# A hybrid attention layer on one core: second weight quarter loaded by rows, square of tile 3 moved to ScalarE, start-up work reordered

## The chip, the core and the metric

The kernel runs on one core of one Trainium2 chip. The metric is the device time of one execution in microseconds, median over repeated runs.

## What is computed

One decoder layer on x of 512 x 1024 (float32), cut to what matters:

```python
h = rmsnorm(x, norm_pre_g)                      # per row, over 1024
u = h @ w_in                                    # 1024 x 4096
dq, dk, dv, dg, mq, mk, mv, mg = split(u)       # 512 columns each
A = diff_attention(dq, dk, dv, lam, bias)       # 4 heads, two softmax maps, p0 - lam * p1, rmsnorm per head
B = moba_attention(mq, mk, mv, bias)            # 8 heads; at 512 rows all causal blocks are taken
y = concat(A * silu(dg), B * silu(mg)) @ w_out
out = x + rmsnorm(y, norm_post_g)
```

## The kernel before

The rows of x are four tiles of 128 (t = 0 to 3), the 1024 inner columns eight rows of blocks (k = 0 to 7). A unit is one 128 x 512 result of the projections: 32 units for `w_in` and 8 for `w_out`, in the order of the table `ORDER`. Products are made in float16 pairs: each operand is split into a high and a low half (`w_hi`, `w_lo`; `ht[:, 0]`, `ht[:, 1]`), and three products are summed in PSUM (high with high, high with low, low with high). The weights come in quarters of two rows k, 512 KB each, into `stage` (four places): `load_quarter(n)` on SyncE, but the second quarter (n = 1) by ScalarE's queue. ScalarE makes the high half (`split`, L748 and L749), VectorE the low one (L910, L912, or one row with `split_row`, L899). SyncE loads a place again when both halves are made (`split_lo`), and for quarters 4 to 6 also when TensorE has read it (`first_read`).

The start is different for each tile:
- Tile 0 / unit 0 doesn't wait for its norm. TensorE turns the raw rows (L539), VectorE weighs them by the norm's gains (`x_weigh`, L1001), and `first_quarter` (L592) multiplies float32 weights straight from `stage`, quarter by quarter; the factor 1/rms of tile 0 (`first_scale`) is put on at the eviction (`unit(0)`, L771 on ScalarE, L954 on VectorE).
- Tile 1: the square of its left half on ScalarE (`x_square`, L735), of its right half on VectorE (`x_half_square`, L963), their sum on VectorE (`x_mean_square`, L971), its reciprocal root on POOL (L481), `x_norm(1)` on VectorE (L977). TensorE turns the rows after the third quarter of unit 0 (L539, waits for `xs_ready`); ScalarE takes the high half from PSUM (`x_hi(1)`, L788), VectorE the low one (`x_lo(1)`, L1012).
- Tiles 2 and 3: squares, sum and root in the same way, then ScalarE writes the high half of the normed rows (`xn_hi`, L823, waits for the root), VectorE the low one (`xn_lo`, L1018), and SyncE turns each with a DMA transpose (`turn_x`, L400) into `ht`.

Units 1 to 3 run in `late_lower_unit`: 16 matmuls with the high half of the tile (L611), then 8 with the low one (L618), so that the low half is wanted only later. Units from 4 on (`unit_quarter`, L581) want all four tiles. After seven units the attention steps are mixed with further units, in slots set by tables; TensorE then multiplies to the end, and rows are normed and stored.

Within an engine the order is that in which the program is written. On SyncE the first loads are: tile 0, quarter 0, tile 1, quarter 2 (waits for tile 0), quarter 3 (waits for quarter 0), tile 2 (waits for `w_loaded[1]`, the second quarter), tile 3 (waits for tile 1), quarters 4 and 5, then the four transposes (both high halves, then both low ones), quarters 6 to 8. ScalarE's order there is `x_square(0)`, `split(0)`, `x_square(1)`, `split(1)` to `split(3)`, `x_square(2)`, `x_hi(1)`, `x_square(3)`, `xn_hi(2)`, `unit(0)`, `xn_hi(3)`.

Of the kernel before, what the change touches and what calls it, by code (L numbers as in the profile page):

```python
# [7 lines left out]
def bass_hymba_diff_moba_layer(  # L8
# [25 lines left out]
    ALU = mybir.AluOpType  # L34
# [145 lines left out]
    with ctx:  # L180
# [99 lines left out]
        rows_stored = sem("rows_stored")  # L280
        strips_loaded = [sem(f"strips_loaded{r}") for r in range(2)]
        w_loaded = [sem(f"w_loaded{i}") for i in range(4)]
        xres_loaded = [sem(f"xres_loaded{t}") for t in range(TILES)]
        stored = [sem(f"stored{i}") for i in range(2)]
        stored_last = sem("stored_last")
# [72 lines left out]
        def _(sp):  # L358
# [59 lines left out]
            load_quarter(5)  # L418
            with nc.allow_non_contiguous_dma(reason="32 x 12 table, transposed once"):
                sp.dma_start(rel_t, rel_bias.rearrange("b h -> h b")).then_inc(rel_loaded, 16)  # L420
            for h in range(2):
                for t in range(2, TILES):
                    turn_x(t, h)
            load_quarter(6)
            load_quarter(7)
# [44 lines left out]
        @block.gpsimd  # L470
        def _(pool):
            nc.gpsimd.memset(ident[:, :], 0.0).then_inc(ident_zero, 1)
            nc.gpsimd.memset(minus_half[:, :], -0.5).then_inc(consts_ready, 1)
            pool.wait_ge(ident_zero, 1)
            nc.gpsimd.affine_select(out=ident[:, :], in_=ident[:, :], compare_op=ALU.not_equal, fill=1.0,
                                    base=0, pattern=[[-1, P]], channel_multiplier=1).then_inc(consts_ready, 1)
            pool.wait_ge(consts_ready, 2)

            for t in range(TILES):
                pool.wait_ge(x_mean, t + 1)  # L480
                nc.gpsimd.tensor_tensor(x_rstd[:, t:t + 1], x_ms[:, t:t + 1], minus_half[:, 0:1],  # L481
                                        ALU.pow).then_inc(x_rstd_ready, 1)
                if t == 0:
                    pool.wait_ge(x_rstd_ready, 1)
                    nc.gpsimd.tensor_scalar(first_scale[:, :], x_rstd[:, 0:1], U_SCALE, 1.0, ALU.mult,
                                            ALU.mult).then_inc(first_scale_ready, 1)

            nc.gpsimd.memset(row_sb[:, 0:P - 1], MASKED).then_inc(row_masked, 1)
            pool.wait_ge(rel_loaded, 16)
            for b in range(BUCKETS):  # L490
                lo = first_distance(b)
                hi = first_distance(b + 1) if b + 1 < BUCKETS else SEQ + 1
                last = nc.gpsimd.tensor_copy(row_sb[:, P - 1 + lo:P - 1 + hi],
                                             rel_t[:, b:b + 1].to_broadcast([HEADS, hi - lo]))
                if b == BUCKETS - 1:
                    last.then_inc(row_built, 1)
            pool.wait_ge(subln_loaded, 16)


            keep = (1.0 - LAMBDA_INIT) ** 2  # L500
            for c in range(DIFF_HEADS):
                pool.wait_ge(sub_squared, TILES * (c + 1))
                nc.gpsimd.tensor_scalar(sub_ms[:, c, :], sub_sq[:, c, :], 1.0 / (2 * DH * keep),  # L503
                                        SUBLN_EPS / keep, ALU.mult, ALU.add).then_inc(sub_mean, 1)
                pool.wait_ge(sub_mean, c + 1)
                nc.gpsimd.tensor_tensor(sub_rstd[:, c, :], sub_ms[:, c, :], minus_half[:, :],
                                        ALU.pow).then_inc(sub_rstd_ready, 1)
                pool.wait_ge(sub_rstd_ready, c + 1)
                rows = gates[:, 0, :, c * P:(c + 1) * P]
                nc.gpsimd.tensor_tensor(rows, rows, sub_rstd[:, c, :].unsqueeze(2).to_broadcast([P, TILES, P]),  # L510
                                        ALU.mult).then_inc(sub_scaled, 1)
                pool.wait_ge(sub_scaled, c + 1)
                nc.gpsimd.tensor_tensor(rows, rows, subln[:, :].unsqueeze(1).to_broadcast([P, TILES, P]),
                                        ALU.mult).then_inc(diff_normed, 1)

            for t in range(TILES):
                i = t
                pool.wait_ge(y_squared, 2 * i + 1)
                nc.gpsimd.tensor_scalar(y_part[:, t:t + 1], y_sq[:, t, 0:1], NORM_EPS * W_SCALE ** 2, 1.0,
                                        ALU.add, ALU.mult).then_inc(y_part_ready, 1)  # L520
                pool.wait_ge(y_part_ready, i + 1)
                pool.wait_ge(y_squared, 2 * (i + 1))
                if t < TILES - 1:
                    nc.gpsimd.tensor_tensor(y_ms[:, t:t + 1], y_sq[:, t, 1:2], y_part[:, t:t + 1],
                                            ALU.add).then_inc(y_mean, 1)
                else:
                    nc.gpsimd.tensor_tensor(y_most[:, :], y_sq[:, t, 1:2], y_part[:, t:t + 1],
                                            ALU.add).then_inc(y_most_ready, 1)
                pool.wait_ge(y_mean, i + 1)
                nc.gpsimd.tensor_tensor(y_rstd[:, t:t + 1], y_ms[:, t:t + 1], minus_half[:, 0:1],  # L530
                                        ALU.pow).then_inc(y_rstd_ready, 1)
# [3 lines left out]
        def _(pe):  # L535
# [50 lines left out]
            def first_quarter(q):  # L586

                pe.wait_ge(x_first_ready, q // 2 + 1)
                pe.wait_ge(w_loaded[q], 16)
                for k in (2 * q, 2 * q + 1):  # L590
                    cols = slice(k % 2 * WIDTH, (k % 2 + 1) * WIDTH)
                    last = nc.tensor.matmul(unit_ps[:, 0, :], x_first[:, k, :], stage[:, q, cols], start=(k == 0),  # L592
                                            stop=(k == KT - 1))
                last.then_inc(first_read if q < 3 else unit_done, 1)
# [132 lines left out]
        def _(act):  # L727
# [10 lines left out]
            def split(n):  # L738

                g, k = n // 4, 2 * (n % 4)  # L740
                act.wait_ge(w_loaded[n % 4], 16 * (n // 4 + 1))
                if g >= 3:
                    act.wait_ge(unit_done, LAST_OF_GROUP[g - 3] + 1)
                src = stage[:, n % 4, :].rearrange("p (k n) -> p k n", k=2)
                if g < len(GROUPS):
                    if n == 0:
                        act.wait_ge(g_scaled, 1)
                    nc.scalar.activation(w_hi[:, g % 3, k, :], src[:, 0, :], ACT.Copy, scale=g_cols[:, k:k + 1])  # L748
                    nc.scalar.activation(w_hi[:, g % 3, k + 1, :], src[:, 1, :], ACT.Copy,  # L749
                                         scale=g_cols[:, k + 1:k + 2]).then_inc(split_hi, 1)  # L750
                else:
                    nc.scalar.activation(w_hi[:, g % 3, k:k + 2, :], src, ACT.Copy,
                                         scale=W_SCALE).then_inc(split_hi, 1)
# [72 lines left out]
            def x_square(t):  # L826
                act.wait_ge(x_loaded[t], 16)

                square(x_sq[:, t:t + 1], x_sb[:, t, 0:DM // 2], x_squared, t + 1)

            nc.scalar.dma_start(g_rows[:, :], norm_pre_g[0].rearrange("(k p) -> k p", p=P)).then_inc(gpre_loaded, 16)  # L831
            first = GROUPS[0][2]
            nc.scalar.dma_start(stage[:, 1, :].rearrange("p (k n) -> p k n", k=2),
                                w_in_v[:, 2:4, first:first + WIDTH]).then_inc(w_loaded[1], 16)
            x_square(0)
            split(0)
            x_square(1)
# [2 lines left out]
            split(3)  # L840
            x_square(2)
            x_hi(1)
            x_square(3)
            xn_hi(2)
            unit(0)
            xn_hi(3)
            for u in range(1, FIRST_UNITS):
                if u > 2:
# [1 line left out]
                        split(n)  # L850
                    unit(u)
                if u == 1:
                    split(4)
                    unit(1)
                    split(5)
                    x_hi(0)
# [36 lines left out]
        def _(dve):  # L893
            def split_row(n, part):

                g, k = n // 4, 2 * (n % 4) + part
                dve.wait_ge(split_hi, n + 1)
                src = stage[:, n % 4, part * WIDTH:(part + 1) * WIDTH]
                ins = nc.vector.scalar_tensor_tensor(w_lo[:, g % 3, k, :], src, g_cols[:, k:k + 1],  # L899
                                                     w_hi[:, g % 3, k, :], ALU.mult, ALU.subtract)  # L900
# [221 lines left out]
            split(0)  # L1122
            x_half_square(1)
            x_mean_square(1)
            x_norm(1)
            split(1)
            split_row(2, 0)
            x_half_square(2)
            x_mean_square(2)
            split_row(2, 1)  # L1130
            x_half_square(3)
            x_mean_square(3)
            split(3)
            x_lo(1)
            unit(0)
            xn_lo(2)
            xn_lo(3)
            for u in range(1, FIRST_UNITS):
                if u > 2:
# [2 lines left out]
                unit(u)  # L1142
                if u == 1:
                    x_scale()
                    split(4)
                    split(5)
                if u == 2:
                    x_lo(0)
                    split(6)
                if u == 3:  # L1150
                    dve.wait_ge(lam_loaded, 16)
                    dve.wait_ge(x_half_squared, TILES)
                    for i in range(2):
                        nc.vector.tensor_tensor_reduce(out=heads_out[:, i * DH:(i + 1) * DH],
                                                       in0=lam_in[:, 2 * i, :], in1=lam_in[:, 2 * i + 1, :],
# [70 lines left out]
```

## Time and profile before

| | |
|---|---|
| median of 3 runs | 253.86 us (253.48 to 253.91) |
| the profiled execution's own time | 253.41 us |
| its span on the core | 251.6 us |
| granted TensorE clock | 0.997 of full speed |
| busy | TensorE 244.8 us (97%), VectorE 178.4 us (71%), ScalarE 142.9 us (57%), POOL 30.1 us (12%) |
| DMA queues | 42.47 MB, mean 169 GB/s |

The times of single instructions come from the profiled execution, whose span leaves out some 1.8 us around the recorded work. Start times are counted from the start of the span. The ends of matmuls are modelled, and neighbouring matmuls overlap in the records, so that starts say more than durations. PEld is TensorE's weight load; a name with q (SPq) is an engine's queue, here for the instruction that issues a DMA.

### The profile page before, as it was taken

The numbers are of one execution on the slowest core, as the hardware profiler recorded it, in microseconds if no ns is written. First come the engines' busy times: TensorE is split into PE (matmuls) and PEld (weight loads), VectorE is DVE, ScalarE is ACT, GpSimd is POOL, SyncE is SP. The second block draws the span as 40 slices with busy tenths as digits, with TensorE's granted clock in tenths as the row PEclk, the third lists the DMA queues.
The fourth block names the chain that finished last, engine by engine and source line by source line (L and its number), as shares of the span: only waits on it lengthen the run. The fifth ranks groups of instructions, "written<-read, shape, count | busy, mean of one in ns | idle before, by whom it ended". The sixth has DMA issues, their size and how long they took to land.

```text
span 251.6 us, 4449 instructions
## 1 busy us (share of the span) xinstructions
PE 244.8 (97%) x1564; PEld 122.5 (49%) x1564; DVE 178.4 (71%) x396; ACT 142.9 (57%) x336; POOL 30.1 (12%) x73
## 2 busy tenths in 40 slices
PE   8999999999999999999999999999999999999991
PEld 7444444445444554544455444454444444555570
DVE  3899786587477788868777767968788896835313
ACT  3894675274456666574676595577566655611110
POOL 1267000000000410040041032000000000111101
PEclk9999999999999999999999999999999999999998
DMA  7978989605765545443935553577749876982422
GB/s 262 389 225 188 315 261 375 193 5 135 107 182 141 181 115 145 139 157 106 208 96 137 147 161 112 131 199 179 179 102 199 202 182 155 198 208 42 125 86 83
DMA packets 59674, 42.47 MB, mean 169 GB/s; under 512 B 45808, under 2 KB 46072, under 8 KB 59652
## 3 DMA queue, kind: packets, MB, share of 16 engines
q1 hardware_dynamic: 59364, 41.66, 62.0%
q10 hardware_dynamic: 288, 0.53, 0.6%
q8 instruction: 13, 0.21, 0.4%
q14 instruction: 9, 0.07, 0.1%
HBM read 29.04 MB, written 2.13 MB: 124 GB/s over the span
## 4 chain that ended last, share of the span: by engine, by line
PE 94%; DMA 3%; issue 1%; DVE 0%; DVEq 0%; ACTq 0%; ACT 0%; POOLq 0%; POOL 0%
PE unit_ps L581 73%; PE score_ps L637 6%; PE o_ps L658 5%; PE unit_ps L611 4%; DMA stage<-in_w_in_dram 3%; PE unit_ps L592 2%; PE unit_ps L618 2%; PE unit_ps L712 1%; PE score_ps L712 1%; PE score_ps L539 0%; DVE area L1107 0%; DVEq L180 0%; ACTq L831 0%; ACT junk L735 0%; POOLq L180 0%
## 5 line engine op out<-in xcount | busy, mean ns | idle before, releaser
L581 PE MATMUL unit_ps<-area,w_hi 128*128 128x512 f16 x256 | 76.3, 380 | 0.0
L796 ACT ACTIVATE arena<-arena,negmax 128x512 f32<-128x512 f32 (+3 forms) x64 | 35.4, 554 | 50.0 <-DVE negmax L1034 49.9
L581 PE MATMUL unit_ps<-w_hi,area 128*128 128x512 f16 x192 | 60.3, 380 | 0.0
L581 PE MATMUL unit_ps<-area,w_lo 128*128 128x512 f16 x128 | 48.6, 379 | 0.0
L581 PEld LDWEIGHTS unit_ps<-area,w_hi 128*128 128x128 f16 x256 | 24.0, 98 | 27.3 <-issue 1.1
L581 PE MATMUL unit_ps<-w_lo,area 128*128 128x512 f16 x96 | 36.4, 379 | 0.0
L1034 DVE CUSTOM_DVE_ANT_0 arena<-score_ps,strips 128x512 f32<-128x512 f32 (+3 forms) x64 | 28.6, 485 | 9.4 <-PE score_ps L637 9.4
L910 DVE SCALAR_TENSOR_TENSOR w_lo<-stage,g_cols,w_hi 128x512 f16<-128x512 f32 x31 | 23.7, 765 | 10.1 <-ACT w_hi L749 10.1
L581 PEld LDWEIGHTS unit_ps<-w_hi,area 128*128 128x128 f16 x192 | 18.8, 98 | 21.9 <-issue 1.2
L748 ACT ACTIVATE w_hi<-stage,g_cols 128x512 f16<-128x512 f32 x32 | 22.7, 710 | 4.0 <-DMA stage<-in_w_in_dram 4.0
L912 DVE SCALAR_TENSOR_TENSOR w_lo<-stage,g_cols,w_hi 128x512 f16<-128x512 f32 x31 | 24.1, 778 | 0.0
L749 ACT ACTIVATE w_hi<-stage,g_cols 128x512 f16<-128x512 f32 x32 | 22.6, 707 | 0.0
L1063 DVE TENSOR_TENSOR arena<-arena 128x512 f16<-128x512 f32 (+5 forms) x32 | 21.0, 656 | 1.5 <-ACT arena L810 1.5
L810 ACT ACTIVATE arena<-arena 128x512 f16<-128x512 f32 (+5 forms) x32 | 19.0, 592 | 3.6 <-DVE arena L1054 3.5
L581 PE MATMUL unit_ps<-w_hi,q_hi 128*128 128x512 f16 x64 | 19.9, 380 | 0.0
L581 PEld LDWEIGHTS unit_ps<-area,w_lo 128*128 128x128 f16 x128 | 12.5, 98 | 15.1
L658 PE MATMUL o_ps<-v_hi,pt 128*128 128x64 f16 (+1 forms) x240 | 18.9, 202 | 0.0
L658 PEld LDWEIGHTS o_ps<-v_hi,pt 128*128 128x128 f16 x240 | 15.5, 98 | 3.8
L735 ACT ACTIVATE junk<-unit_ps 128x512 f16<-128x512 f32 (+1 forms) x8 | 4.5, 564 | 22.6 <-PE unit_ps L581 22.0
L658 PE MATMUL o_ps<-v_lo,pt 128*128 128x64 f16 (+1 forms) x120 | 16.2, 202 | 0.0
L581 PE MATMUL unit_ps<-w_hi,q_lo 128*128 128x512 f16 x48 | 14.9, 379 | 0.0
L503 POOL TENSOR_SCALAR sub_ms<-sub_sq 128x4 f32<-128x4 f32 x4 | 0.8, 193 | 113.2 <-ACT junk L735 113.2
(114 smaller groups left out, 356.7 us busy)
## 6 DMA issues: line engine op xcount, KB each, us to landing
stage<-in_w_in_dram SPq DMA_DIRECT2D x31, 512.0 KB, 4.0
stage<-in_w_out_dram SPq DMA_DIRECT2D x8, 512.0 KB, 4.2
arena<-in_x_dram SPq DMA_DIRECT2D x4, 512.0 KB, 5.0
strips<-bias_rows SPq DMA_DIRECT2D x4, 512.0 KB, 4.8
stage<-in_x_dram SPq DMA_DIRECT2D x4, 512.0 KB, 4.1
out_dram<-area SPq DMA_DIRECT2D x3, 512.0 KB, 2.7
strips<-bias_rows SPq DMA_DIRECT2D x1, 1024.0 KB, 8.0
stage<-in_w_in_dram ACTq DMA_DIRECT2D x1, 512.0 KB, 6.9
```

Source lines behind the costliest of these rows:

```text
L581: last = nc.tensor.matmul(bank, a, b, start=(k == 0 and n == 0), stop=(k == KT - 1 and n == 2))
L611: nc.tensor.matmul(bank, ht[:, 0, k, rows], b[:, g % 3, k, :], start=(k == 0 and b is w_hi), stop=False)
L637: last = nc.tensor.matmul(score_ps[:, bank, col:col + n], a[part, ch, rows], b[part, ch, 0:n], start=first, stop=final)
L658: last = nc.tensor.matmul(o_ps[:, o % 2, col:col + width], a, b[:, k, src], start=(k == 0 and n == 0), stop=(k == t and n == 2))
L748: nc.scalar.activation(w_hi[:, g % 3, k, :], src[:, 0, :], ACT.Copy, scale=g_cols[:, k:k + 1])
L749: nc.scalar.activation(w_hi[:, g % 3, k + 1, :], src[:, 1, :], ACT.Copy, scale=g_cols[:, k + 1:k + 2]).then_inc(split_hi, 1)
L796: nc.scalar.activation(probs[:, i % 2, m, 0:n], probs[:, i % 2, m, 0:n], ACT.Exp, bias=negmax[:, i, m:m + 1], scale=-1.0, accum_out=sums[: ...
L810: nc.scalar.activation(hi, probs[:, i % 2, 0:1 + r, 0:n], ACT.Copy).then_inc(p_hi_ready, 1)
L910: nc.vector.scalar_tensor_tensor(w_lo[:, g % 3, k, :], src[:, 0, :], g_cols[:, k:k + 1], w_hi[:, g % 3, k, :], ALU.mult, ALU.subtract)
L912: nc.vector.scalar_tensor_tensor(w_lo[:, g % 3, k + 1, :], src[:, 1, :], g_cols[:, k + 1:k + 2], w_hi[:, g % 3, k + 1, :], ALU.mult, ALU.s ...
L1034: nc.vector.tensor_tensor_reduce(out=probs[:, i % 2, m, 0:n], in0=score_ps[:, bank, col:col + n], in1=strips[:, h, 0:n][:, ::-1], scale=-1 ...
L1063: nc.vector.tensor_tensor(lo, probs[:, i % 2, 0:1 + r, 0:n], hi, ALU.subtract)\
```

## The change

- The second quarter is loaded by two DMAs of one row each, both on ScalarE's queue: row 2 counts on `row_loaded`, row 3 on `w_loaded[1]`. TensorE waits for each row by itself. ScalarE's `split(1)` waits for both, and signals its first row by `row_split`.
- VectorE's low half of row 2, `split_row(1, 0)`, runs ahead of `x_norm(1)`, row 3 behind it; quarter 2 is split whole ahead of tile 2's half square.
- The square of tile 3 is made by ScalarE alone over 1024 columns, and POOL adds the epsilon; VectorE's `x_half_square(3)` and `x_mean_square(3)` go.
- ScalarE runs `unit(0)` ahead of `xn_hi(2)`, and `x_square(3)` and `split(4)` ahead of `xn_hi(3)`; VectorE runs `split(4)` between `xn_lo(2)` and `xn_lo(3)`.
- SyncE transposes tile by tile (high and low half of tile 2, then of tile 3).

```diff
@@ SyncE, transposes
-            for h in range(2):
-                for t in range(2, TILES):
+            for t in range(2, TILES):
+                for h in range(2):
                     turn_x(t, h)
@@ POOL
             for t in range(TILES):
+                if t == TILES - 1:
+                    pool.wait_ge(x_squared, TILES)
+                    nc.gpsimd.tensor_scalar(x_ms[:, t:t + 1], x_sq[:, t:t + 1], NORM_EPS, 1.0, ALU.add,
+                                            ALU.mult).then_inc(x_mean, 1)
                 pool.wait_ge(x_mean, t + 1)
@@ TensorE, first_quarter
-                pe.wait_ge(w_loaded[q], 16)
                 for k in (2 * q, 2 * q + 1):
+                    pe.wait_ge(row_loaded if k == 2 else w_loaded[q], 16)
@@ ScalarE, split
+                if n == 1:
+                    act.wait_ge(row_loaded, 16)
                 act.wait_ge(w_loaded[n % 4], 16 * (n // 4 + 1))
...
-                    nc.scalar.activation(w_hi[:, g % 3, k, :], src[:, 0, :], ACT.Copy, scale=g_cols[:, k:k + 1])
+                    row = nc.scalar.activation(w_hi[:, g % 3, k, :], src[:, 0, :], ACT.Copy,
+                                               scale=g_cols[:, k:k + 1])
+                    if n == 1:
+                        row.then_inc(row_split, 1)
@@ ScalarE, x_square
-                square(x_sq[:, t:t + 1], x_sb[:, t, 0:DM // 2], x_squared, t + 1)
+                cols = DM // 2 if t < TILES - 1 else DM
+                square(x_sq[:, t:t + 1], x_sb[:, t, 0:cols], x_squared, t + 1)
@@ ScalarE, start
-            nc.scalar.dma_start(stage[:, 1, :].rearrange("p (k n) -> p k n", k=2),
-                                w_in_v[:, 2:4, first:first + WIDTH]).then_inc(w_loaded[1], 16)
+            nc.scalar.dma_start(stage[:, 1, 0:WIDTH], w_in_v[:, 2, first:first + WIDTH]).then_inc(row_loaded, 16)
+            nc.scalar.dma_start(stage[:, 1, WIDTH:2 * WIDTH], w_in_v[:, 3, first:first + WIDTH])\
+                .then_inc(w_loaded[1], 16)
...
             x_square(2)
             x_hi(1)
+            unit(0)
+            xn_hi(2)
             x_square(3)
-            xn_hi(2)
-            unit(0)
+            split(4)
             xn_hi(3)
@@ VectorE, split_row
-                dve.wait_ge(split_hi, n + 1)
+                if part == 0:
+                    dve.wait_ge(row_split, 1)
+                else:
+                    dve.wait_ge(split_hi, n + 1)
@@ VectorE, start
             x_mean_square(1)
+            split_row(1, 0)
             x_norm(1)
-            split(1)
-            split_row(2, 0)
+            split_row(1, 1)
+            split(2)
             x_half_square(2)
             x_mean_square(2)
-            split_row(2, 1)
-            x_half_square(3)
-            x_mean_square(3)
             split(3)
             x_lo(1)
             unit(0)
             xn_lo(2)
+            split(4)
             xn_lo(3)
```

`split(4)` is taken out of its old place, after unit 1, on both engines.

How VectorE's instructions stand around the norm of tile 1 and the sum of tile 2, before (from the half square of tile 1; ISA is the half square and the read of its sum, `stage` with `w_hi` a split):

```order
L963 ISA heads_out,x_half_sq<-arena 128x512 [waits x_half_squared,x_loaded1]
L963 ISA x_half_sq 128x1
L971 TENSOR_TENSOR x_ms<-x_sq,x_half_sq 128x1 [waits x_half_squared,x_squared]
L977 TENSOR_SCALAR arena<-arena,x_rstd 128x1024 [waits x_rstd_ready]
L910 SCALAR_TENSOR_TENSOR w_lo<-stage,g_cols,w_hi 128x512 [waits split_hi]
L912 SCALAR_TENSOR_TENSOR w_lo<-stage,g_cols,w_hi 128x512
L899 SCALAR_TENSOR_TENSOR w_lo<-stage,g_cols,w_hi 128x512 [waits split_hi]
L963 ISA heads_out,x_half_sq<-arena 128x512 [waits x_half_squared,x_loaded2]
L963 ISA x_half_sq 128x1
L971 TENSOR_TENSOR x_ms<-x_sq,x_half_sq 128x1 [waits x_half_squared,x_squared]
L899 SCALAR_TENSOR_TENSOR w_lo<-stage,g_cols,w_hi 128x512 [waits split_hi]
L963 ISA heads_out,x_half_sq<-arena 128x512 [waits x_half_squared,x_loaded3]
```

The same place in the changed kernel:

```order
L979 ISA heads_out,x_half_sq<-arena 128x512 [waits x_half_squared,x_loaded1]
L979 ISA x_half_sq 128x1
L987 TENSOR_TENSOR x_ms<-x_sq,x_half_sq 128x1 [waits x_half_squared,x_squared]
L915 SCALAR_TENSOR_TENSOR w_lo<-stage,g_cols,w_hi 128x512 [waits row_split]
L993 TENSOR_SCALAR arena<-arena,x_rstd 128x1024 [waits x_rstd_ready]
L915 SCALAR_TENSOR_TENSOR w_lo<-stage,g_cols,w_hi 128x512 [waits split_hi]
L926 SCALAR_TENSOR_TENSOR w_lo<-stage,g_cols,w_hi 128x512 [waits split_hi]
L928 SCALAR_TENSOR_TENSOR w_lo<-stage,g_cols,w_hi 128x512
L979 ISA heads_out,x_half_sq<-arena 128x512 [waits x_half_squared,x_loaded2]
L979 ISA x_half_sq 128x1
L987 TENSOR_TENSOR x_ms<-x_sq,x_half_sq 128x1 [waits x_half_squared,x_squared]
L926 SCALAR_TENSOR_TENSOR w_lo<-stage,g_cols,w_hi 128x512 [waits split_hi]
```

One split now stands between the sum of tile 1 and its norm; between that norm and the half square of tile 2 there are three splits, as before.

ScalarE from the square of tile 2 to the first split of the fifth quarter, before (`v_hi` is the eviction of unit 0, `pt` the high half of a normed tile):

```order
L735 ACTIVATE junk,x_sq<-arena 128x512 [waits x_squared,x_loaded2]
L788 ACTIVATE area<-score_ps 128x8x128 [waits xt_ready]
L735 ACTIVATE junk,x_sq<-arena 128x512 [waits x_squared,x_loaded3]
L823 ACTIVATE pt<-arena,x_rstd 128x1024 [waits x_rstd_ready]
L771 ACTIVATE v_hi<-unit_ps,first_scale 128x512 [waits first_scale_ready,unit_done]
L823 ACTIVATE pt<-arena,x_rstd 128x1024 [waits x_rstd_ready]
L748 ACTIVATE w_hi<-stage,g_cols 128x512 [waits w_loaded0]
```

And in the changed kernel:

```order
L741 ACTIVATE junk,x_sq<-arena 128x512 [waits x_squared,x_loaded2]
L799 ACTIVATE area<-score_ps 128x8x128 [waits xt_ready]
L782 ACTIVATE v_hi<-unit_ps,first_scale 128x512 [waits first_scale_ready,unit_done]
L834 ACTIVATE pt<-arena,x_rstd 128x1024 [waits x_rstd_ready]
L741 ACTIVATE junk,x_sq<-arena 128x1024 [waits x_squared,x_loaded3]
L756 ACTIVATE w_hi<-stage,g_cols 128x512 [waits w_loaded0]
L760 ACTIVATE w_hi<-stage,g_cols 128x512
L834 ACTIVATE pt<-arena,x_rstd 128x1024 [waits x_rstd_ready]
```

The first two stand as they did; the eviction has gone ahead of tile 2's high half, and tile 3's square (now of 1024 columns) and the split ahead of tile 3's.

## Rows read from the trace of the kernel before

**Rows 1.** Busy time by stage: us, each engine's busy us (x instructions), clock, DMA share, GB/s.

```profile
0.00:14.60 14.60, 13.28 (x52) 8.62 (x53) 8.99 (x22) 9.49 (x17) 2.67 (x11) 1.00 0.89 326
14.60:30.00 15.40, 15.40 (x73) 6.96 (x73) 14.47 (x21) 9.89 (x15) 8.04 (x35) 1.00 0.84 223
```

**Rows 2.** Waits of TensorE, whole program: waited for, us in total, times, longest.

```profile
PE unit_ps L546 <- PEq L1214: 0.8, 1, 0.8
PE unit_ps L592 <- DMA stage<-in_w_in_dram: 0.3, 1, 0.3
PE unit_ps L592 <- DVE gates L1001: 0.2, 1, 0.2
```

**Rows 3.** Timeline of TensorE: start us, us, engine, line, tile, xcount [idle before <-releaser].

```profile
6.15 1.95 PE L592 MATMUL unit_ps<-stage,gates 128*128 128x512 f32 x4 [0.24 <-DVE gates L1001]
8.42 3.67 PE L592 MATMUL unit_ps<-stage,gates 128*128 128x512 f32 x8 [0.31 <-DMA stage<-in_w_in_dram]
11.93 1.04 PE L539 MATMUL score_ps<-ident,arena 128*128 128x128 f32 x8
...
12.91 1.88 PE L592 MATMUL unit_ps<-stage,gates 128*128 128x512 f32 x4
...
14.53 0.10 PEld L611 LDWEIGHTS unit_ps<-w_hi,area 128*128 128x128 f16 x1 [0.57 <-ACT area L788]
14.63 0.38 PE L611 MATMUL unit_ps<-w_hi,area 128*128 128x512 f16 x1
...
19.59 0.10 PEld L611 LDWEIGHTS unit_ps<-w_hi,area 128*128 128x128 f16 x1
19.81 0.38 PE L611 MATMUL unit_ps<-w_hi,area 128*128 128x512 f16 x1
```

**Rows 4.** Chain of waits, its first transfer: start us, us, what.

```profile
1.34 6.94 DMA stage<-in_w_in_dram
```

**Rows 5.** Timeline of ScalarE, 12 to 17 us.

```profile
12.85 0.63 ACT L735 ACTIVATE junk<-arena 128x512 f16<-128x512 f32 x1 [0.35 <-DMA arena<-in_x_dram]
...
13.47 1.00 ACT L788 ACTIVATE area<-score_ps 128x1024 f16<-128x1024 f32 x1
...
15.09 1.15 ACT L823 ACTIVATE pt<-arena,x_rstd 128x1024 f16<-128x1024 f32 x1
```

**Rows 6.** Timeline of SyncE's DMA issues.

```profile
4.27 2.14 SPq L373 DMA_DIRECT2D stage<-in_w_in_dram  x2
8.30 0.82 SPq L404 DMA_DIRECT2D arena<-in_x_dram  x2
...
16.26 1.33 SPq L400 DMA_TRANSPOSE area<-pt  x1
```

**Rows 7.** DMA issues at 4.27, 8.30, 16.26 us: KB, us from issue to landing.

```profile
stage<-in_w_in_dram SPq DMA_DIRECT2D x1, 512.0 KB, 5.3
...
arena<-in_x_dram SPq DMA_DIRECT2D x1, 512.0 KB, 4.5
...
area<-pt SPq DMA_TRANSPOSE x1, 3.2
```

**Rows 8.** Timeline of VectorE around the norm of tile 1 and the sum of tile 2.

```profile
10.37 0.76 DVE L977 TENSOR_SCALAR arena<-arena,x_rstd 128x1024 f32<-128x1024 f32 x1 [0.67 <-POOL x_rstd L481]
...
13.02 0.69 DVE L963 CUSTOM_DVE_ANT_0 heads_out<-arena 128x512 f32<-128x512 f32 x1
...
13.82 0.16 DVE L971 TENSOR_TENSOR x_ms<-x_sq,x_half_sq 128x1 f32<-128x1 f32 x1
13.90 0.74 DVE L899 SCALAR_TENSOR_TENSOR w_lo<-stage,g_cols,w_hi 128x512 f16<-128x512 f32 x1
```

**Rows 9.** Timeline of POOL: the reciprocal roots of tiles 1 to 3.

```profile
9.78 0.55 POOL L481 TENSOR_TENSOR x_rstd<-x_ms,minus_half 128x1 f32<-128x1 f32 x1 [2.58 <-DVE x_ms L971]
14.06 0.99 POOL L481 TENSOR_TENSOR x_rstd<-x_ms,minus_half 128x1 f32<-128x1 f32 x1 [3.73 <-DVE x_ms L971]
15.60 0.99 POOL L481 TENSOR_TENSOR x_rstd<-x_ms,minus_half 128x1 f32<-128x1 f32 x1 [0.55 <-DVE x_ms L971]
```

More of the change, by code:

```diff
@@ L282, in bass_hymba_diff_moba_layer @@
         w_loaded = [sem(f"w_loaded{i}") for i in range(4)]
+        row_loaded = sem("row_loaded")
+        row_split = sem("row_split")
         xres_loaded = [sem(f"xres_loaded{t}") for t in range(TILES)]
@@ L852, in _ @@
                 if u == 1:
-                    split(4)
                     unit(1)
@@ L1144, in _ @@
                     x_scale()
-                    split(4)
                     split(5)
@@ L1151, in _ @@
                     dve.wait_ge(lam_loaded, 16)
-                    dve.wait_ge(x_half_squared, TILES)
+                    dve.wait_ge(x_half_squared, TILES - 1)
                     for i in range(2):
```

## The prediction

> **What bounds the kernel now.** I read the table of stages first. In the first 14.6 us TensorE is busy for 13.28 us; from 14.6 to 30.0 us it is busy for all 15.40 us [rows 1], and its whole list of waits has three entries, all before that: 0.8 us at the start, 0.2 us on VectorE and 0.3 us on a DMA, both at L592, the first unit [rows 2]. So from 14.63 us on TensorE sets the time: what moves the start of a later matmul moves the end by as much, and what any other engine gains there is worth nothing unless TensorE waits for it. The change touches the first 25 us.
>
> The list hides how close the waits are, because a matmul's row reaches over the next one (0.38 us long, one started every 0.216 us: 24 of them from 14.63 to 19.81 us). Starts tell more [rows 3]. The first unit's matmuls start every 0.43 us (four of them run from 12.91 to 14.34 and the next work starts at 14.63 = 12.91 + 4 x 0.43). The first quarter, from 6.15 us, is therefore through at 7.87 us, and the second starts at 8.42 us: TensorE really stands still for 0.55 us. It waits for the second quarter, issued by ScalarE's queue at 1.34 us and landed 6.94 us later, at 8.28 us [rows 4].
>
> Two other things end just in time, and they decide this case:
> - Unit 1's first weight load starts at 14.53 us, released by ScalarE's high half of tile 1 (13.47 to 14.47 us); its matmul at 14.63 us is also the moment at which TensorE has come through. ScalarE was late because tile 2's rows landed at 12.85 us, and their square (0.63 us) stands ahead of that half [rows 3, 5].
> - Unit 2's first weight load at 19.59 us needs the transpose of tile 2's upper half. SyncE issued it at 16.26 us, and it took 3.2 us: landed at 19.46 us [rows 3, 6, 7]. The margin is 0.13 us. That transpose waited for xn_hi(2) (15.09 to 16.24 us), which waited for POOL's reciprocal root (ended 15.05 us), which waited for x_ms(2), started by VectorE at 13.82 us [rows 5, 8, 9].
>
> **The second quarter by rows.** The stall of 0.55 us goes if row 2 is there at 7.87 us and row 3 at 8.73 us. The same bytes move beside the same other transfers; row 3 is issued one issue (about 0.4 us) later. I bound row 2's landing between 4.27 us (when tile 0, issued first of all, released SyncE [rows 6]) and 8.28 us. The second and third quarters landed 1.29 us apart (8.28 and 4.27 + 5.3 = 9.57 us [rows 6, 7]), so a half is worth about 0.65 us: I take 7.6 us for row 2, and for row 3 the old 8.28 us, since its last byte has the same traffic ahead of it; its bounds are 7.6 and 8.93 us. The extra issue on ScalarE's queue lies before tile 0 is there. The second quarter is then through at 9.59 us; the third landed at 9.57 us, just in time, and ends at 11.31 us. So TensorE comes 0.55 us sooner to the transposes of tile 1. ScalarE still waits for both rows (split(1) has both waits), behind tile 1's square: nothing changes for it up to split(3).
>
> **What gives it back, twice.** First, VectorE now runs split_row(1, 0) between x_mean_square(1) and x_norm(1), in the 0.67 us in which it waited for POOL's root [rows 8]. That looks free. But look at the root: 0.55 us where VectorE waited (9.78 us), 0.99 us both times when VectorE went on with a split (14.06 us, the split 0.16 us earlier [rows 8], and 15.60 us, behind tile 3's sum) [rows 9]. In the changed kernel the split follows x_ms(1) as the one at 13.90 us follows x_ms(2), so it starts at about 9.62 us and the root at 9.78 us: the same distance, so I take 0.99 us. The root ends at 10.77 instead of 10.33 us, and x_norm(1) runs from 10.81 to 11.57 us: 0.44 us late. The transposes, wanted at 11.38 us, start at about 11.77 us instead of 11.93 us, and TensorE is through with the fourth quarter at 14.46 us instead of 14.63 us: 0.17 us are left of 0.55. The bounds of the root are 0.55 and 0.99 us.
>
> The Trainium skill, SBUF — State Buffer, section "Who interferes with whom", has the rule for it: a VectorE instruction with two inputs in SBUF holds off a GpSimd instruction that reads SBUF. Its section "A bandwidth-pool intuition that's wrong (but worth ruling out)" puts the end of such a block at about 115 ns behind the end of VectorE's instruction. An estimate by it: the root would end at 9.62 + 0.74 + 0.12 = 10.48 us and the delay be 0.15 us. The row of 14.06 us says otherwise: that split ended at 14.64 us, the root at 15.05 us, 0.41 us behind; the row decides.
>
> Second, unit 1 still needs ScalarE's half of tile 1, behind the square of tile 2. Tile 2's load is issued as before when w_loaded[1] is there (8.28 us), 4.5 us to landing [rows 7]: 12.85 us, square, half until 14.47 us, first matmul at 14.63 us. **The gain is 0.** If tile 2 landed sooner ScalarE could begin at 12.50 us; TensorE's own 14.46 us then lets 0.17 us through.
>
> **The term that remains.** VectorE's row of work behind x_norm(1) is as long as before: one split has gone ahead of it and one is added (split(2) whole), so three splits lie between it and the half square of tile 2. All is shifted by 0.44 us: half square from 13.46 instead of 13.02 us, x_ms(2) from 14.26 instead of 13.82 us. Tile 2's rows (12.85 us) and ScalarE's square (about 13.5 us) are there. A split follows again, so the root is 0.99 us, from 14.50 to 15.49 us; xn_hi(2) runs from 15.53 to 16.68 us; the transpose is issued at 16.70 us and lands at 19.90 us at 3.2 us. Matmuls started 0.14 us behind the landing of the second quarter (8.28, 8.42), and a weight load with its matmul started 0.06 + 0.10 us behind ScalarE's half (14.47, 14.53, 14.63): unit 2 starts at 20.04 to 20.14 instead of 19.81 us. Term: +0.23 to +0.33 us; I take **+0.25 us**, and 0 if the root keeps 0.55 us. Since transposes no longer follow so closely behind this one, 3.0 us might do, which gives +0.05 us.
>
> **Edits that cost nothing.** unit(0) ahead of xn_hi(2) on ScalarE fits in the gap: TensorE's unit ends at about 14.6 us, and an eviction of 512 columns (about 0.7 us, like the half square) at 15.3 us, before the root (15.49 us). With an undisturbed root at 15.05 us TensorE would also be 0.39 us further ahead, and the eviction would run from the end of ScalarE's half (14.47 us) to about 15.1 us. Tile 3's square by ScalarE: 1024 columns, 1.15 us by the row of xn_hi(2) [rows 5] for 0.63 us, and 0.7 us less on VectorE; with POOL's added sum, root and split(4) (two of about 0.7 us) ahead of xn_hi(3), its half ends at about 20.5 us and its transpose lands at 23.7 us, wanted by unit 3 at 19.81 + 24 x 0.216 = 24.99 us. Lower half: VectorE ends it at about 21.8 us, landed at 25.0, wanted at 28.4 us. SyncE's order by tiles is no worse: the lower half of tile 2 goes at about 18.9 us. The fifth split comes earlier, quarter 8 is issued sooner, and nobody waits for it. All covers are TensorE's 15.40 us of uninterrupted work.
>
> **Sum.** The profiled execution took 253.41 us (span 251.6): 253.41 - 0.55 + 0.55 (given back) + 0.25 = 253.66 us. It lies 0.45 us under the median of 253.86 us; from the median: **254.1 us**. A measurement of this kernel can tell some 0.2% (0.5 us) from no change.
>
> **Rivals.**
> 1. The forecast, unit 2 late by its transpose, +0.05 to +0.33 us: 253.9 to 254.2 us. Chance 0.57.
> 2. The root isn't stretched, or only by 0.15 us. For: only two long rows, and another cause may have made them. With 0.15 us the transpose of tile 2 lands at 19.61 us and unit 2 is late by at most 0.05 us: 253.9 us. (This is what the Trainium skill's SBUF page, cited above, would make of it.) Without any, x_norm(1) is on time, and if tile 2 also lands earlier, because row 3's semaphore comes before 8.28 us, ScalarE starts at 12.50 us and the gain is 0.35 us at unit 1, of which the eviction ahead of xn_hi(2) and the transpose let some 0.1 us through: 253.7 to 253.9 us. Chance 0.20; with case 1 it makes "no change" 0.77.
> 3. Slower: row 3 becomes the late one. Issued 0.41 us later, it may land at 8.7 us by that issue, or at 8.93 us by half a quarter's 1.29 us. SyncE waits for it before it loads tile 2, so that tile lands 0.4 to 0.65 us later, and unit 1 starts that much later, one for one (the transpose's lateness is then hidden): 254.3 to 254.5 us. It decides from 0.25 us on. For it: that wait is the last one ended before SyncE's issue at 8.30 us. Against: the bytes ahead of row 3 are no more. Chance of over 0.2% slower, with what a late transpose adds: 0.15.
> 4. Faster by over 0.2% needs the whole 0.55 us: tile 2 over 0.5 us sooner, an undisturbed root, and a sooner transpose at once. Chance 0.08.
>
> **Range.** From 253.5 us (case 2 with the spread of the runs below the median, 0.4 us) to 254.6 us (case 3).
>
> **What would show it.** In the changed kernel's profile: no wait of L592 on the stage DMA, the first unit's second quarter from about 7.9 us; the second root 0.99 us long; the transposes of tile 1 started between 11.7 and 11.8 us; unit 1 at 14.6 us, released by ScalarE's half; the first transpose of tile 2 issued at 16.7 us and a gap of 0.2 to 0.3 us in TensorE's starts before 20.1 us; nothing after it. I am wrong if unit 1 starts before 14.4 us or after 14.9 us, or if the gap before unit 2 isn't there, or if TensorE waits at a later unit.

## The result, and the profile after

The changed kernel took 254.74 us (median of 9 runs, 254.53 to 254.96) against 253.52 us for the kernel before (9 runs, 253.44 to 254.45): ratio 1.0040, 95% interval 1.0030 to 1.0051. It is slower by 1.2 us from median to median (0.8 to 1.3 us by the interval), and 254.74 us lies 0.14 us above the range that was given. The profiled execution is the slowest of the nine: 254.96 us, span 253.2 us, 1.6 us longer than the span of before.

The waits of TensorE in the whole program (columns as in [rows 2]):

```profile
PE unit_ps L598 <- DMA stage<-in_w_in_dram: 1.1, 1, 1.1
PE unit_ps L552 <- PEq L1228: 0.8, 1, 0.8
PE unit_ps L617 <- ACT area L799: 0.2, 1, 0.2
```

The wait of L592 (now L598) on the stage has not gone. It has grown from 0.3 to 1.1 us and moved: it was in front of the second quarter, and now it is in front of the first. TensorE's timeline of the start:

```profile
7.60 5.39 PE L598 MATMUL unit_ps<-stage,gates 128*128 128x512 f32 x12 [1.11 <-DMA stage<-in_w_in_dram]
13.06 1.09 PE L545 MATMUL score_ps<-ident,arena 128*128 128x128 f32 x8
...
14.10 1.88 PE L598 MATMUL unit_ps<-stage,gates 128*128 128x512 f32 x4
16.16 0.39 PE L617 MATMUL unit_ps<-w_hi,area 128*128 128x512 f16 x1 [0.17 <-ACT area L799]
```

Against [rows 3] the first quarter starts at 7.60 us instead of 6.15, and the three quarters then run without a gap (12 matmuls in 5.39 us). That is not yet the gain of the row-wise wait: the second quarter was wanted at 7.60 + 4 x 0.43 = 9.32 us and was whole at 9.35 us, so that even a wait for the whole quarter would have cost next to nothing. And unit 1 starts at 16.16 us instead of 14.63: 1.53 us of the 1.6 us. The chain of waits says why (start us, us, what):

```profile
1.74 7.61 DMA stage<-in_w_in_dram
9.35 0.02 issue
9.36 5.08 DMA arena<-in_x_dram
14.45 0.02 issue
14.47 0.03 ACT junk L741
14.49 0.51 issue
15.01 0.19 ACT junk L741
15.19 0.92 ACT area L799
16.11 0.05 issue
16.16 3.63 PE unit_ps L617 x16
```

Row 3 of the second quarter landed at 9.35 us, where the whole quarter had landed at 8.28 us [rows 4]. SyncE waits for it before it loads tile 2, which took 5.1 us and landed at 14.45 us instead of 12.85; its square and ScalarE's half of tile 1 follow, and then unit 1.

Row 3 was not the only late one. Three loads as KB and us to landing: the first quarter (`stage`, SPq, issued at 1.2 us), tile 1 (`arena`, 1.65 us) and row 2 (`stage`, ACTq, 1.34 us):

```profile
stage<-in_w_in_dram SPq DMA_DIRECT2D x1, 512.0 KB, 6.3
arena<-in_x_dram SPq DMA_DIRECT2D x1, 512.0 KB, 7.3
stage<-in_w_in_dram ACTq DMA_DIRECT2D x1, 256.0 KB, 5.9
```

The first quarter, which the change doesn't touch, landed at 7.5 us; ScalarE began its split at 6.04 us before and at 7.49 us now. So this is no matter of which load stands ahead: fewer bytes moved. The stretch from 4 to 7 us, before and then in the changed kernel (columns as in [rows 1]; the last three are clock, DMA share, GB/s of the whole core):

```profile
4.00:7.00 3.00, 2.76 (x16) 2.20 (x17) 2.26 (x7) 1.69 (x4) 0.64 (x2) 1.00 1.04 406
```

```profile
4.00:7.00 3.00, 2.49 (x14) 2.30 (x14) 1.83 (x6) 0.72 (x2) 0.14 (x1) 1.00 0.93 312
```

406 - 312 = 94 GB/s over 3 us are 0.28 MB, or 0.7 us at 406 GB/s. The DMA engines are still busy most of the time (share 0.93 for 1.04), but move a quarter less.

The part of the forecast on POOL holds to the hundredth. POOL's roots of tiles 1 and 2, and SyncE's first transpose:

```profile
11.23 0.99 POOL L487 TENSOR_TENSOR x_rstd<-x_ms,minus_half 128x1 f32<-128x1 f32 x1 [3.45 <-DVE x_ms L987]
15.95 0.99 POOL L487 TENSOR_TENSOR x_rstd<-x_ms,minus_half 128x1 f32<-128x1 f32 x1 [3.73 <-DVE x_ms L987]
```

```profile
18.14 6.54 SPq L402 DMA_TRANSPOSE area<-pt  x4
```

The root of tile 1 takes 0.99 us for 0.55 [rows 9]. The transpose is issued at 18.14 us and takes 3.1 us to 21.24 us; unit 2 needs it at 16.16 + 24 x 0.216 = 21.34 us and started at 21.36: as unit 1 is so late, this lateness is hidden.

### The profile page after: what moved, and what is told of

Read it like the earlier page. It is cut to its first block, busy times and chain, and to the rows that moved or that the text cites. A ratio compares the mean times of both kernels' runs of the same rounds, so it can differ in the third digit from the quotient of the medians.

```text
span 253.2 us, 4447 instructions
## 1 busy us (share of the span) xinstructions
PE 245.6 (97%) x1564; PEld 123.0 (49%) x1564; DVE 177.5 (70%) x393; ACT 143.4 (57%) x336; POOL 31.6 (12%) x74
## 4 chain that ended last, share of the span: by engine, by line
PE 91%; DMA 5%; issue 1%; ACT 1%; ACTq 0%; DVE 0%; DVEq 0%; POOLq 0%; POOL 0%
PE unit_ps L587 72%; PE score_ps L643 6%; PE o_ps L664 5%; PE unit_ps L617 4%; DMA stage<-in_w_in_dram 3%; PE unit_ps L624 2%; DMA arena<-in_x_dram 2%; PE unit_ps L718 1%; PE score_ps L718 1%; ACT area L799 0%; DVE area L1123 0%; ACT junk L741 0%; DVEq L180 0%; ACTq L843 0%; ACTq L845 0%
```

## The experiments

Ratios are against the kernel before, run on the same chip.

**Which half of the change costs.** e1 is the kernel before with the loading by rows and the waits on it alone; this is the edit of the load:

```diff
-            nc.scalar.dma_start(stage[:, 1, :]..., w_in_v[:, 2:4, ...]).then_inc(w_loaded[1], 16)
+            nc.scalar.dma_start(stage[:, 1, 0:WIDTH], w_in_v[:, 2, ...]).then_inc(row_loaded, 16)
+            nc.scalar.dma_start(stage[:, 1, WIDTH:2 * WIDTH], w_in_v[:, 3, ...]).then_inc(w_loaded[1], 16)
```

> The kernel before with the second quarter loaded by two DMAs of one row and the waits on them, and no other edit. Theory L (the loading form is the cost: the two DMAs disturb the first transfers, all land 0.9 to 1.6 us late, and tile 2's landing sets unit 1's start): DMA traffic dips between 5.0 and 6.5 us as in the changed kernel, the first quarter lands near 7.5 us instead of 6.0, tile 2 near 14.4 instead of 12.85 us, unit 1 starts near 16.1 us, +1.2 to +1.5 us. Theory O (the reordering of VectorE, ScalarE and SyncE is the cost): within 0.2 us of the kernel before.

Measured: 254.39 us against 253.69, ratio 1.0032 (1.0021 to 1.0042). In its profile the first quarter landed at 7.0 us and tile 2 at 13.66 us, and unit 1 started at 15.35 us:

```profile
4.00:7.00 3.00, 2.33 (x14) 2.14 (x14) 1.99 (x6) 0.73 (x3) 0.31 (x1) 1.00 1.00 312
```

```profile
15.35 0.39 PE L612 MATMUL unit_ps<-w_hi,area 128*128 128x512 f16 x1 [0.15 <-ACT area L791]
```

The same 312 GB/s. The direction and the mechanism are those of theory L, but the size, +0.7 us (0.5 to 1.1 us by the interval), is under the +1.2 us that it named.

e2 is the changed kernel with that load whole again (the diff of e1, reversed, in the changed kernel).

> The changed kernel with the second quarter loaded by one DMA again; all the reordering stays. Theory L: 0 to +0.3 us against the kernel before, unit 1 at 14.6 us, and unit 2 up to 0.3 us late by its transpose, as predicted (second root 0.99 us, transpose issued at 16.7 us). Theory O: +1.0 to +1.3 us.

Measured: 253.80 against 253.69 us, ratio 1.0001 (0.9992 to 1.0010); theory O falls. The reordering costs nothing that can be measured, traffic from 4 to 7 us is 397 GB/s, and the profile shows the term that was forecast. It also shows the first three quarters without a gap (12 matmuls in 5.42 us from 6.73 us), although the second one is loaded and waited for whole: the first quarter began 0.58 us later than before, so that the second was there when it was wanted. POOL's roots of tiles 1 and 2, SyncE's first transpose, TensorE before unit 2:

```profile
10.06 1.03 POOL L486 TENSOR_TENSOR x_rstd<-x_ms,minus_half 128x1 f32<-128x1 f32 x1 [2.24 <-DVE x_ms L983]
14.82 0.99 POOL L486 TENSOR_TENSOR x_rstd<-x_ms,minus_half 128x1 f32<-128x1 f32 x1 [3.73 <-DVE x_ms L983]
```

```profile
17.02 6.55 SPq L401 DMA_TRANSPOSE area<-pt  x4
```

```profile
18.15 1.89 PE L623 MATMUL unit_ps<-w_hi,area 128*128 128x512 f16 x8
20.24 0.38 PE L616 MATMUL unit_ps<-w_hi,area 128*128 128x512 f16 x1 [0.20 <-issue]
```

Eight matmuls of 0.216 us from 18.15 us end at 19.88 us; unit 2 starts at 20.24: a gap of 0.36 us behind a transpose issued at 17.02 us with 3.1 us to landing (20.12 us).

**Is it the number of loads, their size, or what they read?** e7 adds one load of 4 KB behind the whole second quarter, on the same queue.

```diff
+            nc.scalar.dma_start(spare[0:KT, :], norm_pre_g[0]...).then_inc(spare_loaded, 16)
```

> The kernel before with one more load of 4 KB on ScalarE's queue behind the second quarter (the norm's gains once more, into a spare tile). It adds a load and its completion but no bytes to speak of. If the number of loads is the cause: +0.8 us and a dip at 5 to 6 us. If it is the form by rows: within 0.3 us of before.

Measured: 253.75 against 253.69 us, ratio 0.9990 (0.9975 to 1.0004), 402 GB/s from 4 to 7 us. One more load and its completion, as small as this one, cost nothing.

e4 moves row 3 to SyncE's queue; e5 leaves both rows on ScalarE's and issues row 3 only after tile 0 has landed, at 4.2 us; e6 loads the first quarter by rows (SyncE's queue) and the second one whole.

> The kernel before with row 2 by ScalarE's queue and row 3 by SyncE's, behind tile 1. If what costs is that ScalarE's queue has two transfers beside SyncE's: tile 1 and the first quarter land as before (8.1, 6.0 us) and the time is within 0.3 us of the kernel before. If any loading by rows costs: +0.8 to +1.5 us.

> The kernel before with the second quarter by rows on ScalarE's queue, but row 3 issued only after tile 0's square (at about 4.6 us), so that no more than four loads are under way at once, as in the kernel before. If the number of loads under way in the first 4 us is what costs: no dip of the traffic at 5 to 6 us, first quarter landed near 6.0 us, time within 0.3 us of before or better. If a load of one row (256 KB, one 2 KB piece per partition) is itself slow: the dip stays and the time is 0.8 us or more over before.

> The kernel before with the first quarter (SyncE's queue) loaded by two DMAs of one row each and the second one whole. If any loading by rows costs, wherever it stands: a dip again and +0.5 us or more. If only a second load on ScalarE's queue beside SyncE's costs: within 0.3 us of before.

Measured: e4 254.74 us, 1.0043 (1.0030 to 1.0055); e5 254.45 us, 1.0018 (1.0004 to 1.0031); e6 255.02 us, 1.0045 (1.0031 to 1.0060), all against 253.69 us. Each has its dip: 190 GB/s in the sixth us in e4, 180 in e5, in e6 already 266 in the fifth. It comes on either queue and for either quarter. e5 doesn't settle the number of loads under way: from 4.2 us on it has five (first quarter, row 2, tile 1, third quarter, row 3) where the kernel before has four, not four as its expectation says. e11, below, does. The theory in e5's expectation that was right on the dip asked for 0.8 us or more; the interval gives 0.1 to 0.8 us.

The dip does not follow every load of one row, though. In e5 row 3 moves alone on ScalarE's queue (q10) between 7.5 and 9 us, nearly all of its 0.26 MB, and the traffic is whole; from 10.5 to 11.5 us, when row 3 has landed (9.99 us) and nothing moves on q10, it falls once more:

```profile
DMA packets 304, 0.62 MB, mean 411 GB/s; under 512 B 8, under 2 KB 8, under 8 KB 304
q10 hardware_dynamic: 119, 0.24, 41.0%
```

```profile
DMA packets 70, 0.15 MB, mean 148 GB/s; under 512 B 14, under 2 KB 14, under 8 KB 70
```

Row 3 moves without a dip in e1 (408 GB/s from 6.5 to 8.5 us) and in the changed kernel too (407 GB/s from 7 to 9 us). A second dip with no load of one row under way stands in e1 (147 GB/s from 11.0 to 11.5 us), e4 (246 in the twelfth us) and e6 (205 in the tenth) as well. In e4 tile 1 landed on time (8.15 us), and it didn't help: row 3 landed at 8.85 us, and unit 1 started at 15.40 us. e6's profiled run, its slowest at 257.16 us, also had TensorE's granted clock at 0.5 (1.2 GHz) from 9 to 12 us, after it had waited 1.9 us for the stage.

e10 divides another load of 512 KB in the same way: tile 1 in two halves of 512 columns, one 2 KB piece per partition, 4 KB apart in memory.

> The kernel before with tile 1 of x loaded by two DMAs of 512 columns (256 KB each, one 2 KB piece per partition, as a row of weights, but pieces 4 KB apart in memory instead of 16 KB). If a 256 KB load of one 2 KB piece per partition is slow whatever it reads: traffic dips to 200 to 270 GB/s somewhere between 5 and 8 us and +0.5 us or more. If the dip hangs on the weights' 16 KB distance: no dip, within 0.3 us of before.

Measured: 253.71 against 253.74 us, ratio 0.9993 (0.9981 to 1.0005). From 4 to 7 us:

```profile
4.00:7.00 3.00, 3.00 (x15) 2.88 (x16) 1.79 (x6) 1.95 (x4) 0.10 (x1) 1.00 1.01 378
```

So 256 KB in one 2 KB piece per partition are not slow as such: 378 GB/s, at least 363 in each us of that stretch, and no time lost.

e11 divides the second quarter again in two loads of 256 KB, by columns: both rows in each.

```diff
+            for c0, done in ((0, row_loaded), (WIDTH // 2, w_loaded[1])):
+                nc.scalar.dma_start(stage_kn[:, :, c0:c0 + WIDTH // 2],
+                                    w_in_v[:, 2:4, first + c0:first + c0 + WIDTH // 2]).then_inc(done, 16)
```

> The kernel before with the second quarter by two DMAs of 256 KB each that hold half of the columns of both rows (two 1 KB pieces per partition). If what costs is a load of one row only (all its pieces 16 KB apart): no such dip, at most what smaller pieces cost, within 0.5 us of before. If any division of the quarter into 256 KB loads costs: a dip at 5 to 6 us and +0.8 us or more.

Measured: 253.80 against 253.74 us, ratio 1.0006 (0.9992 to 1.0020). e11 differs from e1 in two things: what addresses a load reads, and that it has two pieces of 1 KB per partition. e12 separates them: rows again, but each row goes to the stage in two separated pieces (`pieces` is a view "p (c k n) -> p k c n" with c=2, k=2).

```diff
+            for k, done in ((0, row_loaded), (1, w_loaded[1])):
+                nc.scalar.dma_start(pieces(stage[:, 1, :])[:, k],
+                    w_in_v[:, 2 + k, first:first + WIDTH].rearrange("p (c n) -> p c n", c=2)).then_inc(done, 16)
```

> As e1, the second quarter by two loads of one row each on ScalarE's queue, but every row goes to the stage as two separated pieces of 256 columns, so that each load has two 1 KB pieces per partition, as many and as small as in e11; only the memory addresses differ from e11 (one row, all partitions 16 KB apart, instead of two rows in turn). If the addresses are what costs: traffic from 4 to 7 us near 310 GB/s as in e1 and +0.5 to +1.0 us. If the small number of pieces per load is (8 for each of the 16 DMA engines): near 380 GB/s as in e11 and within 0.3 us of before.

Measured: 254.37 against 253.79 us, ratio 1.0019 (1.0006 to 1.0032). The stage from 4 to 7 us, e11 and then e12:

```profile
4.00:7.00 3.00, 2.81 (x15) 2.62 (x16) 1.78 (x6) 1.93 (x4) 0.10 (x1) 1.00 1.03 378
```

```profile
4.00:7.00 3.00, 3.00 (x15) 3.00 (x16) 1.67 (x6) 2.03 (x4) 0.10 (x1) 1.00 0.88 295
```

Two loads of 256 KB in 1 KB pieces on the same queue in both; 378 GB/s where a load takes two rows in turn, 295 GB/s where it takes one. e11 has as many loads under way as e1 and e12, so their number isn't it. The engines' waits and reads of the second quarter differ as well, but up to 7 us none of them has begun. So the dip hangs on how the addresses are divided between the two loads: with rows each one reads 128 places 16 KB apart (a row of `w_in` is 4096 x 4 bytes). But such a load isn't slow in itself: row 3 of e12, from 7 to 8.5 us, moved at 391 GB/s for the whole core, as in e5. Why the first of them is caught, no run here shows.

**Halves by partitions.** e3 was meant to test the number of loads: two loads of 64 partitions.

> The kernel before with the second quarter loaded by two DMAs of 64 partitions each, both rows in each, so that the number of DMAs is that of the changed kernel but not their shape; TensorE and ScalarE wait for both. If the mere number of DMAs in flight (a completion in the middle of the stream) is the cause: +0.9 to +1.5 us and the same dip near 5 to 6.5 us. If the form by rows is: within 0.3 us of the kernel before.

Measured: 258.84 against 253.69 us, ratio 1.0186 (1.0167 to 1.0204), much more than either expectation. It doesn't tell the number of loads apart, because it brings a worse thing of its own. TensorE's longest wait:

```profile
PE unit_ps L595 <- DMA stage<-in_w_in_dram: 3.9, 1, 3.9
```

From 5 to 11 us the traffic was 197 to 274 GB/s. TensorE stood for 3.9 us; its granted clock was 0.70 in the eleventh us, 0.5 (1.2 GHz) from 11 to 16 us and back at full speed (2.4 GHz) only from 18 us. The Trainium skill, SBUF — State Buffer, section "Door 1: The DMA port swizzle", says that 64 partitions from 0 or from 64 reach only half of the DMA ports, and gives 196 GB/s for 0 to 63 at 1 MiB. The 197 to 274 GB/s here lie near it, but they are the traffic of all loads together, those of 128 partitions included; no run isolates the ports.

**A try for something faster.** e8 keeps the quarter whole and goes at the landing that unit 1 and unit 2 wait for: tile 1's load is held until the norm's gains are there, tile 2 is loaded ahead of quarter 3, its squares and ScalarE's half of tile 1 are moved up, and the split stays behind the norm of tile 1. e9 also loads quarter 6 ahead of the last transpose.

> A try for a faster kernel: the changed kernel with the second quarter whole, tile 1's load held until the norm's gains are there (so that the second quarter lands ahead of it, near 7.5 us), tile 2 loaded ahead of quarter 3, its squares and ScalarE's half of tile 1 moved up, VectorE's split behind the norm of tile 1 again. By the reading that unit 1 and unit 2 wait for tile 2's landing: unit 1 starts at 14.1 to 14.3 us, unit 2 at 19.3 to 19.5 us, -0.3 to -0.5 us against before. If another transfer becomes the late one instead (quarter 3 for TensorE at 12.4 us): 0 to +0.5 us.

> The kernel of e8 with quarter 6 loaded ahead of the last transpose on SyncE's queue. In e8's profile unit 1 started at 14.45 us (before: 14.63) and half of its runs took 252.8 to 253.0 us, the others 253.5 to 254.5 us; the profiled one of the latter lost 1.2 us at the first scores, where VectorE's low half of k stood behind a split of a quarter that came late. If the late issue of quarter 6 (23.63 us for 22.57 us before) starts that: quarter 6 issued near 22.2 us, no wait at the first scores, nearly all runs at 252.8 to 253.2 us, -0.5 to -0.8 us against before. If the later loads are late for another reason (the strips' load, the lambda load): two groups of runs as in e8, median 253.2 to 254.

Measured: e8 253.53 against 253.69 us, ratio 0.9981 (0.9960 to 1.0003); e9 253.46 against 253.74 us, ratio 0.9988 (0.9972 to 1.0004). In e9's profiled run (252.95 us) unit 1 starts at 13.98 us, 0.65 us sooner than before, and TensorE waits for nothing after the first unit:

```profile
13.98 0.38 PE L618 MATMUL unit_ps<-w_hi,area 128*128 128x512 f16 x1
```

But of its 12 runs only three were under 253.0 us, most lay at 253.2 to 253.7, and one took 255.09. In e8 a slower run was the one profiled (254.49 us), and there the gain was lost later, at the first scores:

```profile
PE score_ps L643 <- DVE k_lo L967: 1.2, 1, 1.2
```

So the expectation for e9, nearly all runs at 252.8 to 253.2 us, missed: the earlier quarter 6 is not the whole of it. Neither kernel is shown to beat the kernel before; both intervals still hold 1.

## Why the prediction was wrong

Point by point:
- **TensorE sets the time from 14.63 us on**: right. A later unit 1 (1.53 us in the changed kernel) came out as 1.6 us of span.
- **The stall of 0.55 us in front of the second quarter goes**: the stall is gone (12 matmuls in one piece from 7.60 us), but not by the mechanism that was forecast. The first quarter started so late that the whole second one was there 0.03 us after it was wanted, and in e2 the stall goes without any loading by rows. So this is no hit.
- **"The same bytes move beside the same other transfers"; row 2 at 7.6 us, row 3 at 8.28 us (bounds 7.6 to 8.93)**: this is the step that failed. Row 2 landed at 7.24 us (1.34 + 5.9), within its bounds, row 3 at 9.35 us, outside them. The bytes were the same, but not the rate: 312 instead of 406 GB/s from 4 to 7 us. I took a load's rate from its bytes, and used the shares of a quarter's 1.29 us as if half a quarter were half a load. e1 and e2 show that the loading by rows alone makes the kernel slower. e7, e10 and e11 show that it is not one load more, nor 256 KB in one piece per partition, nor small pieces; e11 and e12 show that it hangs on dividing by rows and not by columns.
- **Rival 3** had the path right (row 3 late, SyncE holds tile 2 back, unit 1 late one for one) and its price too low: it gave 0.4 to 0.65 us, measured are 1.07 us for row 3 and then another half us, as tile 2 took 5.1 instead of 4.5 us, with traffic down to 295 GB/s in the twelfth us. Its reason against, that "the bytes ahead of row 3 are no more", was the same mistake. Its chance, 0.15, was too small.
- **POOL's root is 0.99 us because a split runs beside it**: right, 0.99 us in the changed kernel and 1.03 us in e2, against 0.55 us in e1, where VectorE waits as before. The 115 ns of the Trainium skill's page that the prediction names don't fit: in the changed kernel the split ended at 11.80 us, the root at 12.22, 0.42 us behind.
- **Unit 2 late by its transpose, +0.25 us**: the mechanism is shown in e2 (root, transpose at 17.02 us, gap of 0.36 us), where the change of the median, 0.11 us, is within its interval. In the changed kernel it is hidden behind the later unit 1.
- **The edits that cost nothing**: nothing in e2 speaks against it.

What stays open: whether the reordering adds to the cost of the loading by rows. By the medians e1 has +0.7 us of the +1.2, but the intervals of the two ratios (1.0021 to 1.0042 and 1.0030 to 1.0051) overlap, and e4, without any reordering, came out at 1.0043. So loading by rows can by itself cost as much as the whole change did. In the profiles unit 1 starts at 15.35 us in e1, 15.40 in e4, 15.42 in e5, 15.61 in e12 and 16.16 in the changed kernel, against 14.63 to 14.91 us in e2, e7, e10 and e11; each is one profiled execution (e6's, held up by the clock as well, has 17.81 us).

The Trainium skill, DMA: Bandwidth & Descriptors, section "Latency and other measured facts", has an entry that I overlooked: rows of memory that stand a large power of two apart are copied slowly, an effect that it puts down, as an inference, to channels of the memory that partitions hit in step. Its figures begin at 512 KiB and are for copies within that memory; here the distance is 16 KB. That there is no dip at 4 KB (e10) or with two rows in turn (e11) would fit it. That row 3, with the same 16 KB, moved in traffic of 391 to 411 GB/s (e12, e5) doesn't. The cause of the dip is not shown.

## What to carry to other kernels

Before you divide a load, don't take the rate of the parts from their bytes; ask also what addresses each part reads, and measure it. Here, with two loads of one weight row each, the core's traffic was 312 GB/s for three us where it had been 406 with one load of both rows, and division by columns of both rows was free. While the queue of loads is full, such a loss can be paid by loads that were not touched (the first quarter landed 1.45 us later in the changed kernel, though not in e12), and the one whose landing releases a chain (here tile 2, held back by a semaphore of the divided load) sets the price. And when a slot on one engine looks idle, look at who works in it on the other side: the split put into VectorE's wait for POOL made the root that it waited for 0.44 us longer.

## What the runs showed that I had not expected

- With a weight quarter divided by rows the traffic of all loads falls to 139 to 213 GB/s in its worst half us between 4 and 6.5 us (e1, e4, e5, e6, e12, the changed kernel). It doesn't with the quarter whole (e2, e7), with tile 1 halved (e10) or with the quarter divided by columns (e11, lowest half us 289).
- The load of the other row, later in the same kernels, moves at 391 to 411 GB/s for the core, and in e1, e4, e5, e6 a second dip comes when no load of one row is under way. So "a load of one row is slow" is not what the runs show.
- Two loads of 64 partitions in place of one of 128 cost about 5 us (e3), with TensorE's clock at 0.5 in their wake.
- Unit 1 started 0.65 us sooner in e9's profiled run, but only three of its twelve runs were about that much faster. In e8's profiled run a quarter that landed at 44.6 us took the gain back at the first scores. So the start of this kernel can't be judged by the start alone.
